# Late gates as pairs of seven half products, ahead of the branches

## The reference

```python
h = rmsnorm(x, norm_mix)
z = h @ w_in                      # ten 256-wide slices, then 4 x 1024 merge gates gl
...                               # branches A, B, C, D from the slices
proj = einsum('blnc,ncd->blnd', branches, w_branch)
gates = sigmoid(gl.reshape(B, L, 4, 1024))
x = x + sum(gates * proj, axis=2) @ w_out
...                               # conv FFN (up, gelu gate, down), then a gated embedding
```

## Time and profile before

| what | value |
|---|---|
| median of 3 runs | 1779.08 us |
| profiled execution, span | 1779.0 us |
| instructions | 30161 |
| PE busy | 1757.3 us (99%) |
| DVE busy | 1027.6 us (58%) |
| ACT busy | 695.1 us (39%) |
| POOL busy | 692.1 us (39%) |
| DMA moved | 193.10 MB, mean 109 GB/s |

### The profile page before, as it was taken

One profiled execution on the slowest core, in us unless ns is written; L12 is line 12 of the kernel. 1 busy time (PEld: TensorE's weight loads), 2 busy tenths in 40 slices (PEclk: granted clock), 3 DMA queues, 4 the chain that ended last, 5 costly groups with the idle time before them and its releaser, 6 DMA issues.

```text
span 1779.0 us, 30161 instructions
## 1 busy us (share of the span) xinstructions
PE 1757.3 (99%) x12649; PEld 1706.4 (96%) x12649; DVE 1027.6 (58%) x1202; ACT 695.1 (39%) x967; POOL 692.1 (39%) x450
## 2 busy tenths in 40 slices
PE   8999999999999999999999999999999999999998
PEld 8999999998778999999999999999999999999998
DVE  6952385824676121221442976777777778775744
ACT  6334424215574121121234554444444443334521
POOL 1332312222113122231034287776777736667021
PEclk9999999999999999999999999999999999999999
DMA  6222212234414121211632322223332285434032
GB/s 226 29 72 72 67 58 81 66 135 134 130 60 175 64 97 48 97 65 68 224 114 98 121 96 97 97 100 112 110 107 97 97 300 178 142 116 146 25 121 98
DMA packets 79080, 193.10 MB, mean 109 GB/s; under 512 B 14402, under 2 KB 31330, under 8 KB 77794
## 3 DMA queue, kind: packets, MB, share of 16 engines
q1 hardware_dynamic: 68002, 167.85, 27.1%
q0 software_dynamic: 4032, 14.68, 2.8%
q10 hardware_dynamic: 6912, 8.65, 1.4%
HBM read 138.67 MB, written 52.58 MB: 108 GB/s over the span
## 4 chain that ended last, share of the span: by engine, by line
PE 94%; DVE 3%; ACT 2%; issue 1%; POOL 1%; DMA 0%; SPq 0%; ACTq 0%; DVEq 0%; POOLq 0%
PE ps L976 34%; PE ps L1479 24%; PE ps L963 11%; PE ps L1527 10%; PE ps L1511 3%; PE ps L1148 2%; PE ps L1061 1%; PE ps L1407 1%; PE ps L1233 1%; PE ps L950 1%; PE ps L1003 1%; PE ps L1267 1%; PE ps L1254 1%; PE ps L1565 1%; DVE Fl L2616 1%
## 5 line engine op out<-in xcount | busy, mean ns | idle before, releaser
L3025 POOL TENSOR_TENSOR Wl<-BIG,Wh 128x512 fp32r<-128x512 f32 x110 | 146.7, 1344 | 115.0 <-ACT Wh L1984 115.0
L976 PE MATMUL ps<-Hh,Uh 128*128 128x352 f32 x864 | 187.5, 325 | 0.3
L976 PE MATMUL ps<-Hh,Ul 128*128 128x352 f32 x864 | 186.1, 323 | 0.0
L2638 DVE TENSOR_TENSOR BIG<-BIG,ps 128x1056 f32<-128x1056 f32 x32 | 40.1, 1254 | 231.5 <-PE ps L976 224.9
L2923 POOL CAST Uh<-BIG 128x1024 fp32r<-128x1024 f32 x27 | 33.1, 1225 | 318.3 <-PE ps L963 201.9
L976 PE MATMUL ps<-Hl,Uh 128*128 128x352 f32 x720 | 155.0, 323 | 0.0
L976 PEld LDWEIGHTS ps<-Hh,Uh 128*128 128x128 f32 x864 | 146.9, 189 | 1.7 <-issue 0.7
L976 PEld LDWEIGHTS ps<-Hh,Ul 128*128 128x128 f32 x864 | 148.3, 188 | 0.0
L2951 POOL TENSOR_TENSOR Ul<-BIG,Uh 128x1024 fp32r<-128x1024 f32 x18 | 46.1, 2571 | 223.8 <-ACT Uh L1911 223.8
L963 PE MATMUL ps<-Hh,Uh 128*128 128x352 f32 x384 | 128.3, 334 | 0.8 <-ACT BIG L1708 0.8
L963 PE MATMUL ps<-Hh,Ul 128*128 128x352 f32 x384 | 123.6, 322 | 0.0
(11 more groups left out here) (434 smaller groups left out, 4891.1 us busy)
## 6 DMA issues: line engine op xcount, KB each, us to landing
BIG<-in_wu SPq DMA_DIRECT2D x44, 512.0 KB, 4.6
hidden<-BIG SPq DMA_DIRECT2D x22, 528.0 KB, 2.7
BIG<-in_wgl SPq DMA_DIRECT2D x20, 512.0 KB, 4.5
BIG<-sums SPq DMA_DIRECT2D x12, 792.0 KB, 4.7
BIG<-in_wd SPq DMA_DIRECT2D x6, 1536.0 KB, 9.6
gates<-BIG ACTq DMA_DIRECT2D x48, 176.0 KB, 2.0
BIG<-in_wz POOLq DMA_DIRECT2D x16, 512.0 KB, 3.8
BIG<-hidden SPq DMA_DIRECT2D x9, 792.0 KB, 4.7
```

Of the source, the lines that this page charges most:

```text
L976: ins = nc.tensor.matmul(psb(3 * out + g), w[wp][:, k], x[xp][k][:, t0:t0 + n], start=(k == 0 and wp == xp), stop=(k == kk - 1 and wp == 1))
L2638: v.tensor_tensor(spans(ACC if n == 0 else sig), spans(sig), slab(m_slot(i, u)), ALU.mult)\
L3025: nc.gpsimd.tensor_tensor(Wl[:, b], src, Wh[:, b].bitcast(F32), ALU.subtract).then_inc(S("w_lo"), 1)
```

## The change

18 of the 20 late gates leave the mixing stage. They are computed as nine pairs, each as seven half products, in a new front stage between GC1 and FB0. Two late gates stay in the mixing stage. In detail:

- The normalized input's rows are used as half blocks; DVE forms four sums of them once and both engines split them. High parts of the sums lie over rows 8 to 15 of the row store, where XD and GC stand, so the rows of XC, XD and GC go to DRAM (`early_rows`) and come back behind the pairs. The weight parts lie over XC's place.
- Per pair, POOL forms four weight sums and seven low parts, ACT seven high parts; PE runs seven products into four PSUM pairs; ACT copies two half rows, DVE makes five adds, ACT two sigmoids, and SP stores two rows in `late_gates`.
- The order behind the pairs is FB, C0, QB, D, C1, IB: QB moves ahead of D, and C0 behind FB. Convolutions and trailing means wait for the rows to come back; the tables of branches C and D are loaded late (all counted by `cd_in`, 144).
- The mixing stage has 32 branch products, two gates in it, and no loop over rounds; gates come from DRAM up to seven products ahead into the eight rows of H, mixed rows go straight into the rows of X, and the rows of x are reloaded when a mixed row's low part is made.

The diff, cut to its core:

```diff
-USERS = ("XC0", "XC1", "XD0", "XD1", "GC0", "GC1", "C00", "C01", "FB0", "FB1", "D0", "D1", "QB0", "QB1", "C10", "C11",
+USERS = ("XC0", "XC1", "XD0", "XD1", "GC0", "GC1", "FB0", "FB1", "C00", "C01", "QB0", "QB1", "D0", "D1", "C10", "C11",
...
+COVER = 2
+PAIRS = (4 * LATE - COVER) // 2
...
 SP
-            sp.dma_start(chist, a["chist"]).then_inc(S("cd_in"), 16)
...
+            sp.wait_ge(S("zw_lo"), len(ZW_PIECES))
+            pair_weights(0, "gw_first")
...
+            keep_rows(0, XC)
+            sp.wait_ge(S("stored"), outs)
+            sp.sem_inc(S("raw_stored"), 1)
             sp.wait_ge(S("xc_done"), 4)
...
             out("pool_p", Z[:, XD:XD + 2, SEQ - HIST:SEQ])
+            keep_rows(1, Z[:, XD:XD + 2, :])
             sp.wait_ge(S("stored"), outs)
             sp.sem_inc(S("raw_stored"), 1)
...
+            def gate_out(c, half):
+                sp.wait_ge(*upto("g_sig", 2 * c + half + 1))
+                sp.dma_start(late_gates[2 * c + half], GY[:, half]).then_inc(on(f"g_stored{half}"), 16)
+
+            for c in range(PAIRS - 1):
+                if c and c + 2 < PAIRS:
+                    sp.wait_ge(*upto("gw_lo", 7 * (c + 1)))
+                    pair_weights(c + 2, f"gw_in{c % 2}")
+                gate_out(c, 0)
+                gate_out(c, 1)
...
+            sp.wait_ge(*upto("gp_done", 7 * PAIRS))
+            rows_back(0, XC)
+            sp.dma_start(wrg, a["wrg"]).then_inc(S("cd_in"), 16)
...
+            gate_out(PAIRS - 1, 1)
+            sp.wait_ge(*upto("g_stored1", 16 * PAIRS))
+            sp.dma_start(chist, a["chist"]).then_inc(S("cd_in"), 16)
...
+            for s in range(6, 32):
+                if s >= 14:
+                    if s % 4 == 2 and s // 4 < KD:
+                        branch_weights(s // 4)
+                    sp.wait_ge(S("m_added"), s - 7)
...
+                gate_in(s)
 PE
             block_z("GC1")
-            pe.wait_ge(S("cd_in"), 96)
+            def gate_product(c, b):
+                pe.wait_ge(*upto("gw_lo", split_of(c, b)))
+                if c == 0 and b in S_SPLIT:
+                    pe.wait_ge(*upto("s_lo", S_SPLIT[b]))
...
+                elif b == B21:
+                    pe.wait_ge(*upto("g_copied", 2 * c + 1))
...
+                for k in range(KH):
+                    for w, x in ((Wh, xh), (Wh, xl), (Wl, xh)):
+                        for g in range(2):
+                            ins = nc.tensor.matmul(pair(gate_pair(c, b))[:, g], w[:, b, k],
+                                                   x[:, k, g * QUARTER:g * QUARTER + QUARTER],
...
+            for c in range(PAIRS):
+                for part in ORDER:
+                    gate_product(c, part)
+            block_z("FB0")
+            block_z("FB1")
+            pe.wait_ge(S("cd_in"), 144)
             for g in range(2):
                 unit(f"C0{g}", wrg[:, 0, g], cX[:, 0], 1)
-            block_z("FB0")
-            block_z("FB1")
+            block_z("QB0")
+            block_z("QB1")
             for i in range(2):
                 unit(f"D{i}", wpool[:, i], Z[:, XD + i], 3 + i)
-            block_z("QB0")
-            block_z("QB1")
             for g in range(2):
                 unit(f"C1{g}", wrg[:, 1, g], cX[:, 1], 2)
...
 ACT
+            for c in range(PAIRS):
+                if c:
+                    weight_high(c, B22)
+                    gate_sig(c - 1, 1)
+                    act.wait_ge(*upto("g_stored1", 16 * c))
+                act.wait_ge(*upto("gp_done", made(c, B11)))
+                nc.scalar.activation(quarters(GY[:, 1, HALF:T]), pair(gate_pair(c, B11)), ACT.Copy)\
...
             for i in range(2):
-                z_out(f"GC{i}", Z[:, GC + i, :])
-            act.wait_ge(S("lam_steps"), 3)
+                act.wait_ge(S("cd_ready"), i + 1)
+                z_out(f"FB{i}", FB[:, i])
             rates(0)
             decay(0)
-            act.wait_ge(S("raw_stored"), 1)
-            z_out("FB0", FB[:, 0])
-            act.wait_ge(S("cd_ready"), 2)
-            z_out("FB1", FB[:, 1])
+            for i in range(2):
+                z_out(f"QB{i}", QB[:, i])
             for i in range(2):
                 act.wait_ge(S("cd_done"), 3 + i)
...
             root(0)
             gelu(0)
-            for i in range(2):
-                z_out(f"QB{i}", QB[:, i])
             rates(1)
 DVE
+            sum_made(T1, x21, x22, ALU.add)
+            sum_made(T3, x11, x21, ALU.subtract)
+            sum_made(T2, x22, x11, ALU.subtract)
+            sum_low(T3)
+            sum_made(B22, x12, x11, ALU.subtract)
+            for part in (T2, T1, B22):
+                sum_low(part)
...
+            for c in range(PAIRS):
+                for part in (T2, T3, T1, T4, B22):
+                    gate_sum(c, part)
-            dve.wait_ge(S("cd_in"), 96)
+            dve.wait_ge(S("cd_in"), 144)
...
 POOL
+            gate_sums(0)
+            gate_third(0)
+            split(3, True)
+            for part in LOWS:
+                gate_low(0, part)
+            for c in range(1, PAIRS):
+                gate_low(c, B11)
+                gate_sums(c)
...
+            for s_ in range(2):
+                pool.wait_ge(*upto("gw_lo", 7 * PAIRS))
+                pool.dma_start(uraw[:, s_], a["wz"][s_ + 6]).then_inc(S(f"raw_in{s_}"), 16)
```

More of the change, by code:

```diff
@@ L703, in _ @@
             sp.wait_ge(S("a_pv"), 15)
-            branch_weights(0, 0)
+            branch_weights(0)
             sp.wait_ge(S("as_pv"), 1)
[L706 to L751, removed]
+            for half in range(2):
+                sp.wait_ge(*upto(f"g_stored{half}", 16 * PAIRS))
@@ new lines, in _ @@
+            for s in range(EARLY):
+                gate_in(s)
+            branch_weights(1)
+            sp.wait_ge(S("m_added"), 3)
+            gate_in(5)
+            branch_weights(2)
+            sp.wait_ge(S("m_gate"), COVER)
+            for s in range(6, 32):
[3 more added lines that the diff above has]
+                    sp.wait_ge(S("m_added"), s - 7)
+                if s == 24:
+                    for half in range(2):
+                        sp.dma_start(uraw[:, half], a["wo"][half]).then_inc(S(f"uw_in{half}"), 16)
+                gate_in(s)
@@ new lines, in gate_sig @@
+            def gate_sig(c, half):
+                act.wait_ge(*upto("g_sum", 5 * c + 4 + half))
+                if half == 0:
+                    act.wait_ge(*upto("g_copied", 2 * c + 2))
+                nc.scalar.activation(GY[:, half], GY[:, half], ACT.Sigmoid).then_inc(on("g_sig"), 1)
+            act.wait_ge(S("zc_done"), 2)
+            act.wait_ge(S("raw_stored"), 1)
+            for part in ORDER:
+                weight_high(0, part)
+            act.preload_act_table_set("sigmoid_and_others")
@@ new lines, in _ @@
+            z_out("GC0", gc_rows[0])
+            act.wait_ge(S("raw_stored"), 2)
+            sum_high(T3)
+            sum_high(T2)
+            act.wait_ge(*upto("gw_lo", split_of(0, B22)))
+            act.wait_ge(*upto("gc_kept0", 16))
+            sum_high(T1)
+            z_out("GC1", gc_rows[1])
+            sum_high(B22)
+            for c in range(PAIRS):
+                if c:
+                    weight_high(c, B22)
[3 more added lines that the diff above has]
+                nc.scalar.activation(quarters(GY[:, 1, HALF:T]), pair(gate_pair(c, B11)), ACT.Copy)\
+                    .then_inc(on("g_copied"), 1)
+                if c + 1 < PAIRS:
+                    for part in (B11, T2, T3):
+                        weight_high(c + 1, part)
+                act.wait_ge(*upto("gp_done", made(c, B21)))
+                if c:
+                    act.wait_ge(*upto("g_stored0", 16 * c))
+                else:
+                    act.wait_ge(*upto("gc_kept1", 16))
+                nc.scalar.activation(quarters(GY[:, 0, 0:HALF]), pair(gate_pair(c, B21)), ACT.Copy)\
+                    .then_inc(on("g_copied"), 1)
+                if c + 1 < PAIRS:
+                    for part in (B21, T1):
+                        weight_high(c + 1, part)
+                gate_sig(c, 0)
+                if c + 1 < PAIRS:
+                    weight_high(c + 1, T4)
@@ L1929, in tile_high @@
             def tile_high(r, half):
[L1931 removed]
+                act.wait_ge(S(f"uw_in{half}"), r * 16 + 48)
                 nc.scalar.activation(Uh[:, half], uraw[:, half], ACT.Copy).then_inc(S("late_hi"), 1)
[L1934 to L1948 removed]
+            act.wait_ge(S("a_pv"), 16)
@@ L2937, in _ @@
+            for r_ in range(4, ZB + FILLS):
                 split(r_)
```

491 lines of the change are left out of this document (314 added, 177 removed).

## The result

The changed kernel takes **1783.24 us** (median of 12 runs, 1780.57 to 1786.68) against 1779.19 for the kernel before on the same chip (12 runs): a ratio of 1.0019, 95% interval 1.0010 to 1.0028. It is a little slower; forecast were 1770.0 and a range of 1756 to 1780. The gain in TensorE's work is there, and the joints around it took it back and 4 us more.

What follows compares the result with a forecast made beforehand. TensorE, busy 99% of the span, was taken as the bound. Its work at -25.3 us, plus joints of +5.5, +1.5, +7.0 and +2.3, summed to -9.0, giving 1770.0 us; range 1756 to 1780.

Steps and rivals of the forecast that it cites:

- Removed, added, the pairs: TensorE's work: 18 gates leave the mixing, nine pairs come in, their stores and preparation hidden; net -25.3 us.
- Rival D: In the pairs: waits for stored rows overrun the slack eight times, +9 us, 1779, no change; chance 0.08.
- Front start: Start of the pairs behind GC1: TensorE waits for T2's operand, +5.5 us, ends 2 and 10.
- the rule of the exclusion: Front: VectorE's two-SBUF-input operations and GpSimd's SBUF reads block each other; could add 3.9 us, total about 1774.
- Behind the gates: Between pairs and C01: convolutions start late behind reloaded rows and tables, so C01 waits; +1.5 us, ends 0 and 4.5.
- A cover that moves: Before IB0: QB no longer hides root, gelu and scan, so IB0 waits for C10's sigmoid; +7.0 us, ends 5 and 9.
- Mixing: Mixing stage: 32 products at 2.92 us each, VectorE's work and SP's loads hidden; only its end costs.
- B: Mixing: a GpSimd weight part blocks VectorE once per four products, seven times, +5.5 us, 1775.5; chance 0.07.
- C: Mixing: SP's loads land one after another and bind it, +42 us, 1812; chance 0.13.
- end: End of the mixing: VectorE prepares the first output weights without a gate as cover; +2.3 us, ends 1 and 4.
- Rival A: The joints cost nothing: stores land early, table work is done before IB0 asks; 1756 us, chance 0.12.

Runs made afterwards that it cites:

- e1: Changed kernel with GpSimd splitting GC1's weights ahead of pair 0's four weight sums instead of behind them; 1787.78 us, ratio 1.0042.
- e3: Changed kernel with ScalarE's first root, gelu and sigmoid table load between the two QB copies, not behind D's copies; 1774.89 us, ratio 0.9984.
- e8: e7 plus eight matmuls of constants ahead of pair 0's T2, results unread; 1761.45 us, ratio 0.9899.
- e4: Changed kernel with matmuls of constants, results unread, filling most of TensorE's waits before GC1, C01, IB0 and the output product; 1777.78 us, ratio 0.9993.
- e7: Changed kernel with four moves: GC1's split and T2's parts first, convolution tables early, root and gelu early, output weights split early; 1760.04 us, ratio 0.9888.
- e2: e1 plus T2's high part ahead of T3's on ScalarE and its low part first behind VectorE's four sums; 1780.04 us, ratio 1.0007.
- e5: Changed kernel with the three small convolution and pooling tables in their own place and loaded at the start; 1776.82 us, ratio 0.9983.
- e9: e7 with GpSimd holding back pair 0's third low part (T3's) until VectorE has made T2's; 1764.32 us, ratio 0.9923.

## Why the prediction failed

**Removed, added, the pairs: right.** 1512 matmuls took 185.25 us (184.6 forecast), no wait inside, stored rows landing in 2.7 us. Rival D is out.

**Front start: wrong, +5.5 against 10.2.** The step looked for the wait at T2 and took GC1's end, 82.75, as given. GC1 is where TensorE waited, 7.5 us: GpSimd's split of GC1's weights stands behind pair 0's sums, and those wait for XC's rows in DRAM, which landed 13.9 us after their issue. The prediction said that GpSimd "now splits GC1's weights and pair 0's beside VectorE", priced VectorE's slowdown and did not ask in which order GpSimd works. Nor did it price GpSimd's own slowdown: four sums and the split took 17.4 us here (61.94 to 79.32), and with 1.29 a sum and 1.03 and 2.38 for a split that meets no work of VectorE (290.33, 280.37) they come to 8.6. TensorE was free for GC1 at 71.9, so by this estimate an undisturbed GpSimd would not have kept it waiting even in the wrong order; e1 shows that the right order is enough. The wait at T2 was real; e1 brought it to light, and larger than forecast (8.7 against 5.5): the landing was nearly right (82.7 against 81), but VectorE's three operations behind it took 2.5, 3.4 and 3.3, not 2.36. There the rule of the exclusion, which the prediction weighed and set aside, was the better price.

**Behind the gates: mis-sized, +1.5 against a wait of 5.5.** The mechanism was right. VectorE began 12.0 us behind the pairs (11 forecast) and ended its second convolution 17.2 later (15.3 forecast). Four of its operations were lengthened beside GpSimd's splits, by some 5.5 us together (the kernel before had such places too, and the 15.3 holds them). The start, one of the four, and the same operation later with GpSimd idle:

```profile
290.58 0.82 DVE L2532 COPY BIG<-BIG 128x24 f32<-128x24 f32 x1 [11.29 <-DMA BIG<-in_wpool]
291.52 2.87 DVE L2535 TENSOR_SCALAR BIG<-BIG,par 128x1024 f32<-128x1024 f32 x1
...
299.57 0.81 DVE L2535 TENSOR_SCALAR BIG<-BIG,par 128x1024 f32<-128x1024 f32 x1
```

**A cover that moves: right**, 7.1 against 7.0, by the release forecast, and e3 confirms the cause.

**Mixing: right.** TensorE waits for single operands, under 1 us each, so B and C did not come at their prices. Something of C is there all the same: the branch weights' load that landed after 10.3 us (4.5 was read from the earlier trace rows) is on the chain that ends last; TensorE's wait at its end is 0.2 us here, 1.9 in e1 and 1.8 in e8. At its **end** the wait rose from 0.6 to 3.1, 2.5 against 2.3.

**What no step held: the restart.** The prediction priced each wait at its length and put what follows it at nothing. It cost 8.2 us in the traced execution, a share at each joint; e4 gave 7.7 of them back there, and 5.5 by the medians. With 8.2 the forecast would have been 1778. Of the rest the waits hold 2.4 at the front (10.2 - 2.3 - 5.5) and 4.0 at C01; the stretch from IB0 to the mixing gave 2.6 back (1.2 and the 1.4 of its restart), and the traced execution of the kernel before had a restart of its own there. That trace held the warning: the rows read ahead of the prediction took the matmuls' spacing from long undisturbed stretches, and no row was read of how TensorE goes on behind a wait.

Rival A, that the joints cost nothing, is what e7 comes near to: 1760 against its 1756.

## What to carry to other kernels

Where TensorE is the bound, a wait costs its length and may cost a restart behind it: here 1.4 to 2.3 us at the lower clock behind each wait of 5 to 7.5 us, and 2.5, 1.5 or nothing behind one of 3.1. A change that makes several short waits is priced with that at each; and a gain of 25 us is lost at the joints sooner than in the work. When an engine gets new work, write its whole list in the new order and ask what each old step now stands behind. Waits hide one behind the other: remove one and look again before counting it as gained.

## What the runs showed of the hardware

The clock behind a wait: the waits of 5.2 to 7.5 us before GC1, C01 and IB0 were followed by slow matmuls in every trace that has them unfilled (GC1 13.69 to 13.94 us, C01 3.60 to 3.86, IB0 24.91 to 25.38). Behind the wait of 3.14 us before the output product they were not always. It stands, with the same code around it, in the changed kernel and in e1, e2, e3 and e5. The 144 matmuls behind it took 25.96 in the changed kernel; in e3 and e2:

```profile
867.85 24.99 PE ps L1549 x144
```

```profile
873.28 23.46 PE ps L1549 x144
```

In e1 and e5 they took 23.46 as well. So in three of the five the clock stayed at its upper level, and what decides it is not shown.

The clock can also fall while TensorE is working again: behind the wait of 2.2 us in e9 some nine matmuls of T2 came 0.122 apart and only then others 0.22 apart.

Ten useless matmuls ahead of a product saved 2.5 us there (e4). Two engines with no data in common went in step at 3.4 us per operation for more than 20 us (e2, e7), and e9 shows the one that started later waiting.
